# Up matrices of the experts issued by ScalarE instead of SyncE, in a two-layer encoder with mixture of experts

## The reference

```python
def block_fn(args):                    # rows of one expert e
    xb = x_pad[rows]
    h = jax.nn.silu(xb @ w_gate[e]) * (xb @ w_up[e])
    return h @ w_down[e]
```

## Time and profile before

| | |
|---|---|
| median of 3 runs | 1155.81 us (1154.29 to 1155.97) |
| the profiled execution | 1156.6 us, span 1154.4 us |
| granted clock of TensorE, mean | 0.891 |
| PE busy | 869.6 us, 75% |
| DVE busy | 235.9 us, 20% |
| ACT busy | 168.7 us, 15% |
| DMA | 439.26 MB, mean 381 GB/s |
| SyncE's queue (q1) | 433.96 MB, 90.3% of the 16 engines |
| ScalarE's queue (q10) | 1.04 MB, 0.3% |

### The profile page before, as it was taken

How to read it: one execution, slowest core, us unless ns; L and a number is a source line. 1 busy time by engine, 2 the same in 40 slices (tenths; PEclk the granted TensorE clock), 3 DMA queues, 4 the chain that set the end, 5 groups by cost and what they waited for, 6 DMA issues and landing times.

```text
span 1154.4 us, 20158 instructions
## 1 busy us (share of the span) xinstructions
PE 869.6 (75%) x9103; PEld 503.1 (44%) x9103; DVE 235.9 (20%) x777; ACT 168.7 (15%) x458; POOL 42.7 (4%) x48
## 2 busy tenths in 40 slices
PE   8999996656686657656899999986575675666566
PEld 4454663424344434334444555644242452434244
DVE  2350421111002111101234435211110111111111
ACT  1141210101011000101224232111010110101011
POOL 1551000000000000000000000000000000000000
PEclk9999897878779887888999999998798888878898
DMA  9993899999999999999982258999999999999996
GB/s 347 329 329 153 326 426 427 426 428 426 427 426 427 427 427 427 426 427 429 394 332 102 118 219 364 401 425 426 428 427 428 426 427 426 427 428 426 428 426 283
DMA packets 46261, 439.26 MB, mean 381 GB/s; under 512 B 4640, under 2 KB 5888, under 8 KB 21600
## 3 DMA queue, kind: packets, MB, share of 16 engines
q1 hardware_dynamic: 43632, 433.96, 90.3%
q0 software_dynamic: 1088, 2.97, 1.1%
q10 hardware_dynamic: 1456, 1.04, 0.3%
HBM read 436.91 MB, written 1.05 MB: 379 GB/s over the span
## 4 chain that ended last, share of the span: by engine, by line
DMA 51%; PE 44%; DVE 2%; ACT 1%; issue 1%; SPq 0%; POOL 0%; DVEq 0%
DMA mem<-in_moe_w_up 44%; PE psum L1344 39%; DMA mem<-in_moe_w_down 7%; PE psum L1484 2%; PE psum L1476 1%; PE psum L1499 1%; DMA mem<-in_ev_w_in 1%; PE psum L1365 0%; PE psum L1408 0%; DVE mem L995 0%; PE psum L1351 0%; ACT mem L675 0%; DVE mem L1145 0%; DVE mem L1141 0%; PE psum L1658 0%
## 5 line engine op out<-in xcount | busy, mean ns | idle before, releaser
L1344 PE MATMUL psum<-mem 128*32 128x256 f32 (+3 forms) x7114 | 668.4, 436 | 260.8 <-DMA mem<-in_moe_w_up 226.8
L1344 PEld LDWEIGHTS psum<-mem 128*32 128x32 f32 (+2 forms) x7114 | 346.1, 131 | 554.3 <-issue 457.6
L1042 DVE TENSOR_TENSOR mem<-psum,mem 128x128 f32<-128x128 f32 x62 | 18.1, 292 | 642.7 <-ACT mem L689 642.7
L689 ACT ACTIVATE mem<-psum 128x128 f32<-128x128 f32 x62 | 17.2, 278 | 518.5 <-PE psum L1344 518.5
L1484 PE MATMUL psum<-mem 32*128 32x256 f32 x1024 | 73.3, 400 | 2.9 <-ACT mem L695 1.9
L1344 PE MATMUL psum<-mem,x 128*128 128x128 f32 (+1 forms) x512 | 63.7, 285 | 7.2 <-DVE mem L995 3.7
L1344 PEld LDWEIGHTS psum<-mem,x 128*128 128x128 f32 x512 | 62.0, 202 | 8.8 <-DVE mem L995 4.5
L1484 PEld LDWEIGHTS psum<-mem 32*128 32x128 f32 x1024 | 46.2, 184 | 30.6 <-issue 23.4
L1003 DVE TENSOR_SCALAR mem<-cst,mem 128x128 f32<-128x128 f32 x124 | 37.2, 343 | 20.6 <-PE psum L1476 20.6
L695 ACT COPY mem<-psum 128x256 f32<-128x256 f32 x62 | 23.1, 373 | 97.0 <-PE psum L1344 97.0
L691 ACT COPY mem<-psum 128x256 f32<-128x256 f32 x62 | 23.1, 373 | 64.0 <-PE psum L1476 63.9
(11 more groups left out here) (180 smaller groups left out, 315.3 us busy)
## 6 DMA issues: line engine op xcount, KB each, us to landing
mem<-in_moe_w_gate SPq DMA_DIRECT2D x64, 2048.0 KB, 47.7
mem<-in_moe_w_up SPq DMA_DIRECT2D x64, 2048.0 KB, 47.6
mem<-in_moe_w_down SPq DMA_DIRECT2D x62, 2048.0 KB, 43.3
mem<-in_od_w_in SPq DMA_DIRECT2D x6, 2048.0 KB, 22.3
mem<-in_ev_w_in SPq DMA_DIRECT2D x3, 2048.0 KB, 19.3
mem<-in_ev_w_out SPq DMA_DIRECT2D x2, 2048.0 KB, 28.2
mem<-in_od_w_out SPq DMA_DIRECT2D x2, 2048.0 KB, 19.4
mem<-in_moe_w_down SPq DMA_DIRECT2D x2, 1536.0 KB, 41.9
```

The costliest lines, as they stand in the source:

```text
L689: nc.scalar.activation(M["sg"], bank(4)[:, 0:P], ACT.Silu).then_inc(s["silu"], 1)
L1042: link(V.tensor_tensor(M["h"], src, M["sg"], ALU.mult))
L1344: return nc.tensor.matmul(out_, lhsT, rhs, start=start, stop=stop)
```

## The change

The two functions that issue a piece move out of SyncE's program and get the issuing engine as a parameter. A rule, `on_act`, picks the up pieces from n = 11 on whose slot last held a down piece, outside place 16 and outside the pieces whose slot last held one of place 16. SyncE skips them. ScalarE issues them, each right behind its copy of y of the expert four places earlier; it takes no further wait, since the wait ahead of that copy is the one that SyncE had.

```diff
+        def load(eng, l, kind, e, to):
+
+            name, rows = (("moe_w_gate", DC), ("moe_w_up", DC), ("moe_w_down", DN_ROWS))[kind]
+            return eng.dma_start(to.rearrange("p (e f) -> p e f", e=1),
+                                a[name][l, bass.ds(e, 1)].rearrange("e (p r) f -> p e (r f)", r=rows))
+
+        def expert_piece(eng, ph, l, n):
+
+            p, kind = divmod(n, 3)
...
+            load(eng, l, kind, p if p < LOOP_AT else p - 1, piece_slot(ph, n)).then_inc(arrived[ph, n][0], 16)
+
+        def on_act(n):
+
+            return n % 3 == 1 and n >= SLOTS and LOOP_AT not in (n // 3, (n - SLOTS) // 3)
+
...
             for n in range(PIECES):
                 if n // 3 == LOOP_AT:
                     if n % 3 == 0:
                         last_and_more("B", 0)
+                    continue
+                if on_act(n):
                     continue
...
-                expert_piece("B", 0, n)
+                expert_piece(sp, "B", 0, n)
...
                     act.wait_ge(used[ph], 3 * place(e) + 3)
                     nc.scalar.copy(M["y"], bank(5)[:, 0:COLS]).then_inc(s["y"], 1)
+                    n = 3 * place(e) + 2 + SLOTS
+                    if n < PIECES and on_act(n):
+                        expert_piece(act, ph, l, n)
```

More of the change, by code:

```diff
@@ L434, in build @@
         block = ctx.enter_context(nc.Block())
+        def load(eng, l, kind, e, to):
[4 more added lines that the diff above has]
+            p, kind = divmod(n, 3)
+            if n == PIECES - 1:
+                rows = a["moe_w_down"][l, p - 1].rearrange("(p r) f -> p r f", r=DN_ROWS)
+                to, most = piece_slot(ph, n).rearrange("p (r f) -> p r f", r=DN_ROWS), DN_ROWS - 1
+                eng.dma_start(to[:, 0:most], rows[:, 0:most]).then_inc(s_hd, 16)
+                eng.dma_start(to[:, most:DN_ROWS], rows[:, most:DN_ROWS]).then_inc(arrived[ph, n][0], 16)
+                return
+            load(eng, l, kind, p if p < LOOP_AT else p - 1, piece_slot(ph, n)).then_inc(arrived[ph, n][0], 16)
+        def on_act(n):
+            return n % 3 == 1 and n >= SLOTS and LOOP_AT not in (n // 3, (n - SLOTS) // 3)
         @block.sync
@@ L454, in _ @@
                     sp.dma_start(cst[:, C_TRI:C_COMMON], a["c_common"][:, C_TRI:C_COMMON]).then_inc(s_load["cst"], 16)
[L456 to L471, removed]
             def last_and_more(ph, l):
@@ L484, in last_and_more @@
                     for kind in range(3):
-                        load(l, kind, e, piece_slot(ph, n0 + kind)).then_inc(s["more_landed"], 16)
+                        load(sp, l, kind, e, piece_slot(ph, n0 + kind)).then_inc(s["more_landed"], 16)
             for n in range(PIECES):
@@ L552, in _ @@
                     sp.wait_ge(used["D"], n - SLOTS + 1)
-                expert_piece("D", 1, n)
+                expert_piece(sp, "D", 1, n)
             for g in (0, 2):
```

## The result

| | before | after |
|---|---|---|
| median | 1155.67 us (14 runs, 1154.12 to 1159.91) | 1159.55 us (14 runs, 1157.81 to 1164.47) |
| ratio | | 1.0037, 95% interval 1.0026 to 1.0049 |
| profiled execution | 1156.6 us, span 1154.4 | 1157.91 us, span 1155.8 |

The change makes the kernel slower by 0.37%, 4.3 us with 3.0 to 5.7 as its interval. The prediction said 1160.9 us and 5.1 us slower.

The account below looks back on a forecast made before the run. Bound by the 16 DMA engines for 779 us of streams, by TensorE between them. Terms 0 + 0 + 2.7 + 2.4 = +5.1 us on the median of 1155.81 gave 1160.9 us; range 1154.0 to 1168.0, 8 in 10.

Parts of the forecast that it names:

- The issue on ScalarE: ScalarE's 52 issues of 0.35 us fit into the 3.08 us idle ahead of the next silu; cost 0.
- The rate: In both streams two queues feed the same 16 engines at an unchanged rate: 0, bounds 11.7 us either way.
- rivals 1 and 3: In the streams, two queues carry more (1149.2 us, chance 0.12), or hinder each other (1172.6 us, chance 0.11).
- rival 3: Alternating between two tensors costs stream rate, or the looped expert lets engines run dry: 1172.6 us, chance 0.11.
- The order of the landings: Ups overtake SyncE's queue, landing within some 10 us; the last gate lands where the last up did; stream's end stays.
- Rival 2: No overtaking: the last up lands after the last gate and the stream-end handovers stay; 1155.8 us, chance 0.17.
- The tail: At each stream's end, TensorE's last-expert work runs behind the later gate: +2.7 us in layer 0, +2.4 in layer 1.
- Depth at the loop: At the looped expert, 9 transfers or 44 us under way cover 30.9 us without freed slots, some 13 us spare: 0.
- The clock: In each layer's tail, TensorE's lower clock, or an unfinished expert before, could make it up to 3 us longer.

Follow-up runs that it names:

- e1: The changed kernel with the last up matrix of each layer left on SyncE's queue, the 50 others on ScalarE's; 1.0010, 1155.58 us.
- e2: The kernel before with only the last up matrix of each layer issued by ScalarE; 1.0037, 1160.08 us.
- e3: The changed kernel, all 52 ups on ScalarE's queue, with the last expert's up half done before its gate half; 1.0011, 1157.29 us.
- e7: The changed kernel with the last expert's combine and gates' transposes ahead of the wait for its gate; 1.0020, 1158.12 us.
- e10: The changed kernel with two extra matmuls in the wait ahead of the expert before the last, gate half still first; 1.0061, 1161.87 us.
- e6: The kernel before with each layer's last up on ScalarE's queue and the last expert's up half first; 1.0020, 1158.70 us.
- e8: The kernel before with each layer's last up on ScalarE, last expert's up half first, four extra matmuls before the last-but-one expert; 0.9996, 1154.95 us.
- e9: The changed kernel with the last expert's up half first and two extra matmuls ahead of the expert before the last; 0.9999, 1155.36 us.
- e11: The kernel before with four extra matmuls in the wait ahead of the expert before the last; 0.9989, 1154.31 us.
- e4: The changed kernel with the three ups under way over the looped expert (pieces 52, 55, 58) kept on SyncE's queue; 1.0044, 1160.23 us.
- e5: The changed kernel with the last expert's up half first and the three ups over the looped expert on SyncE's queue; 1.0003, 1156.71 us.

## Why the prediction was right, point by point

*The issue on ScalarE, 0.* Right. Its 52 issues took 0.33 to 0.35 us each, and the silu behind one kept its 3.08 us of idle time:

```profile
153.61 0.37 ACT L703 COPY mem<-psum 128x256 f32<-128x256 f32 x1 [1.52 <-PE psum L1355]
153.62 0.33 ACTq L440 DMA_DIRECT2D mem<-in_moe_w_up  x1
157.07 0.28 ACT L697 ACTIVATE mem<-psum 128x128 f32<-128x128 f32 x1 [3.08 <-PE psum L1355]
```

*The rate, 0.* Right: 427 GB/s in the stream's windows with one queue and with two, which takes rivals 1 and 3 (as to rate) out. The other half of rival 3, that the looped expert lets the engines run dry, came about in small; see below on depth. e1 bounds what 50 matrices on the second queue cost at 0.25%.

*The order of the landings.* Right in what landed when. A median of 14.9 us, not "within some 10", was the time from issue to landing; it changed nothing. Rival 2, no overtaking, is out: the ups overtook, and with them the tail came.

*The tail, +2.7 and +2.4.* Right in mechanism and place, by e1, e2, e3 and e7. Measured as stream lengths it is 2.8 and 2.7 us after the change, 3.0 and 2.8 in e2. The term of layer 1 was 0.3 us short, since the last gate landed 0.3 us later in its stream than the last up had (419.76 after 419.42), which the forecast had put at nothing; e2, without dips, has it too (419.90). That the whole lies in the range says less: from 1154.0 to 1168.0 us it was wide enough for rival 2. The lengths of the streams are what bears the mechanism out.

*Depth at the loop, 0.* The step that was wrong, in its reasoning: I held the stretch without a freed slot at 30.9 us and found 13 us to spare. It grew to 36.2 us, and to 43.7 on SyncE alone. The looped expert's own three matrices stand in SyncE's queue behind the delayed gates and downs. It had all of them without a wait before and began at 337.03; now TensorE reaches it later and waits for its down matrix:

```profile
349.20 5.97 PE L1355 MATMUL psum<-mem 128*32 128x256 f32 x64 [3.85 <-DMA mem<-in_moe_w_down]
```

The engines ran partly dry, worth 0.6 us a layer of their time in that profile and 1.6 in e10's. I had not followed the looped expert's own matrices through the new order. That the term still measured 0.1 us or less in the changed kernel's profile is luck, not the 13 us to spare; in layer 0 of e10 it was about 1.5.

*The clock.* I had put it into the range as "3 longer a layer". That is what e6 shows: the lower clock costs 2.9 us in the gate_up of the last but one expert, and 2.6 us of stream 0 (e6 against e8). In the changed kernel's own profile the same gate_up took 3.66 us in both layers.

The sum of the streams, +5.4 us, lies 0.3 above the forecast of 5.1, from one profile of each kernel; the ratio's 4.3 lies 0.8 under it and its interval holds both.

## What to carry to other kernels

Here a stream of loads bounded the kernel, and moving some to another queue changed the order in which they landed (14.9 us from issue to landing, not 47.6) and not the rate. Where you do the same, ask of the last piece of each stream what now stands behind it in the engine's program: the 3.4 us of work that used to run while the last up was on its way had nothing left to hide behind once that landed early. Turning the program's order with the landings took most or all of the loss away where the clock held (e3, e8, e9). And a matrix that lands early fills a slot: count the depth with every consumer's own loads in the new order, not with the old stretches.

## What the runs showed that I had not expected

ScalarE's issue of a transfer started at the same moment as the copy ahead of it in its program (153.62 against 153.61, and within 0.01 us in all 52), not behind its 0.37 us. The issue of 0.33 to 0.35 us ends before the copy. "Behind its copy of y" is the place in the program, not a delay.

Four matmuls of no use in a wait, 3.7 us in all, made a kernel 2.8 us faster as the ratios have it (0.9996 against 1.0020, of 1155; the intervals just touch): after 6.07 us of waiting TensorE ran gate_up at a granted clock of 0.50, after 2.28 us, with those matmuls ahead of it, in the 3.66 us that it takes at 1.00. Elsewhere two or four such matmuls did not clearly pay: 1.0061 in e10, 0.9989 with 1 inside the interval in e11.

The wait ahead of the last but one expert's gate_up does not settle its clock by its length alone. After 0.8 to 2.3 us of waiting it took 3.66 us in all seven cases of the profiles. After 2.8 to 3.1 us it took 3.66 in seven and 4.93 to 6.51 in three (layer 0 of e4, both layers of e5). After 4.1 to 7.8 us it took 4.94 to 6.56 in all eight. So one profile of a kernel, or one good tail, does not say what its other executions do.

The stretches outside the streams, with the same instructions, differed by 2.35 and 1.68 us between two profiled executions. In the first stretch the clock was seen at 0.50 in one and 1.00 in the other.
